# Attention scores as products of short operands, and a triangular inverse from blocks of 4, in a three-block network

## The reference

```python
def compress(kv, pe, w1, w2):
    blocks = (kv[:, blk] + pe).reshape(B, nc, CMP_LEN * NSA_KV_DIM)
    return jax.nn.silu(blocks @ w1) @ w2
...
s_w = (jnp.einsum('bnqhd,bnkd->bnhqk', q.reshape(B, n_qb, Q_BLOCK, H, dh), kw).astype(f32) * scale
       - slopes[None, None, :, None, None] * dist[None, :, None].astype(f32))
p_w = masked_softmax(s_w, mask[None, :, None])
...
s = jnp.einsum('bqhid,bkhid->bhiqk', qb, k).astype(f32) * scale
```

```python
r_t, w_t, k_t, v_t, a_t, b_t = inp
sa = jnp.einsum('bhvk,bhk->bhv', S, a_t)
S = S * w_t[:, :, None, :] + sa[..., :, None] * b_t[:, :, None, :] + v_t[..., :, None] * k_t[:, :, None, :]
y = jnp.einsum('bhvk,bhk->bhv', S, r_t)
```

## Time and profile before

| | |
|---|---|
| median of three runs | 4650.26 us (4645.92 to 4656.61) |
| profiled execution | 4649.78 us, span 4648.0 us |
| mean granted clock of PE | 0.957 |
| PE busy | 4284.1 us, 92% of the span |
| DVE, ACT, POOL busy | 41%, 29%, 25% |
| compress stage | 441.4 to 470.1 us |
| NSA attention | 470.1 to 682 us |
| diff attention | 682 to 868 us |
| recurrence, first to last right side | 1507.7 to 1904.0 us |

### The profile page before, as it was taken

One profiled execution on the slowest core, in us unless ns is written; L12 is line 12 of the kernel. 1 busy time (PEld: TensorE's weight loads), 2 busy tenths in 40 slices (PEclk: granted clock), 3 DMA queues, 4 the chain that ended last, 5 costly groups with the idle time before them and its releaser, 6 DMA issues. The chain is left out here.

```text
span 4648.0 us, 53906 instructions
## 1 busy us (share of the span) xinstructions
PE 4284.1 (92%) x21558; PEld 3501.7 (75%) x21558; DVE 1886.4 (41%) x3289; ACT 1343.2 (29%) x2357; POOL 1154.4 (25%) x575
## 2 busy tenths in 40 slices
PE   8999999879995888699999999999999999967897
PEld 6888777656775887468888877888788888856776
DVE  3022666652595665435424424000133333346433
ACT  3121333432313443421001012112244444343112
POOL 2220100331152666222222212212111111122313
PEclk9999999879997999899999999999999999978899
DMA  3243111331523110311111112333333333266422
GB/s 123 102 157 102 34 27 26 118 97 50 208 87 99 42 31 17 110 46 46 55 46 46 55 37 89 113 138 104 90 84 104 104 107 95 67 218 191 154 82 91
DMA packets 276997, 417.23 MB, mean 90 GB/s; under 512 B 50439, under 2 KB 184120, under 8 KB 270862
## 3 DMA queue, kind: packets, MB, share of 16 engines
q1 hardware_dynamic: 221022, 313.20, 21.8%
q10 hardware_dynamic: 53104, 94.92, 5.5%
q0 software_dynamic: 2624, 5.68, 0.5%
HBM read 290.31 MB, written 123.40 MB: 89 GB/s over the span
## 5 line engine op out<-in xcount | busy, mean ns | idle before, releaser
L163 POOL TENSOR_TENSOR weights_wlow<-weights_raw,weights_whigh 128x1024 fp32r<-128x1024 f32 (+1 forms) x236 | 695.6, 2969 | 2450.3 <-ACT weights_whigh L154 2450.3
L154 ACT ACTIVATE weights_whigh<-weights_raw 128x1024 fp32r<-128x1024 f32 (+1 forms) x236 | 266.6, 1164 | 1170.8 <-PE acc L313 787.8
L313 PE MATMUL acc<-h_high_half,weights_whigh 128*128 128x512 f32 x1408 | 556.8, 395 | 20.9 <-POOL weights_wlow L163 17.1
L313 PE MATMUL acc<-h_low_half,weights_whigh 128*128 128x512 f32 x1408 | 553.7, 393 | 0.0
L313 PE MATMUL acc<-h_high_half,weights_wlow 128*128 128x512 f32 x1408 | 553.5, 393 | 0.0
L313 PEld LDWEIGHTS acc<-h_high_half,weights_whigh 128*128 128x128 f32 x1408 | 266.0, 189 | 89.2 <-POOL weights_wlow L163 18.4
L3575 PE MATMUL acc<-h_high_half,weights_whigh 128*128 128x512 f32 x768 | 331.3, 431 | 0.0
L313 PEld LDWEIGHTS acc<-h_high_half,weights_wlow 128*128 128x128 f32 x1408 | 265.9, 189 | 59.3 <-issue 1.0
L313 PEld LDWEIGHTS acc<-h_low_half,weights_whigh 128*128 128x128 f32 x1408 | 265.6, 189 | 59.3
L3575 PE MATMUL acc<-h_low_half,weights_whigh 128*128 128x512 f32 x768 | 302.2, 393 | 0.0
L3575 PE MATMUL acc<-h_high_half,weights_wlow 128*128 128x512 f32 x768 | 300.8, 392 | 0.0
(11 more groups left out here) (555 smaller groups left out, 8238.9 us busy)
## 6 DMA issues: line engine op xcount, KB each, us to landing
weights_raw<-w_cols SPq DMA_DIRECT2D x94, 512.0 KB, 4.8
weights_raw<-w_ff SPq DMA_DIRECT2D x64, 512.0 KB, 3.7
weights_raw<-w_rows SPq DMA_DIRECT2D x30, 1024.0 KB, 7.2
att<-gated_result_sb SPq DMA_DIRECT2D x96, 130.0 KB, 2.2
merge_o_sb<-att SPq DMA_DIRECT2D x24, 520.0 KB, 6.6
rows<-norm_square ACTq DMA_DIRECT2D x48, 256.0 KB, 2.1
weights_raw<-w_out SPq DMA_DIRECT2D x24, 512.0 KB, 3.8
cols<-first_out ACTq DMA_DIRECT2D x40, 256.0 KB, 2.0
```

Source lines behind the costliest of these rows:

```text
L154: self.core.nc.scalar.activation(high[p][:, half * (KC // 2):(half + 1) * (KC // 2), :], raw[half], ACT.Copy).then_inc(self.core.sem("roun ...
L163: self.core.nc.gpsimd.tensor_tensor(low[p][:, hs, :], raw[half], high[p][:, hs, :].bitcast(F32), ALU.subtract).then_inc(self.core.sem("wei ...
L313: mm = nc.tensor.matmul(core.acc[b][:, :], wt[p][:, k, c * P:(c + 1) * P], h[:, k, half * HALF:(half + 1) * HALF], start=first, stop=final)
```

## The change

**Scores.** Queries and keys of both attentions are rounded to fp32r ("short"), and what the rounding drops (the "low") is kept as a second short operand. q k is then q_high k_high + q_high k_low + q_low k_high, and the three terms lie below each other on the rows of the operands. In NSA (head size 64) a chunk takes two products: [q_high; q_high] with [k_high; k_low] on 128 rows, and [q_low; slope, slope] with [k_high; two parts of the position] on 66. In diff (head size 32) a chunk takes one, of 3 x 32 + 6 = 102 rows. The masks and the identity in front of them are short too. Turn, mix and softmax stay as they are.

The rows are made by loading the same columns two or three times. In `compress` the clearing of the loaded tiles is gone; ACT rounds keys and masks (`round`) when all loads are there, between its Silus of i = 0 and i = 1, and the compressed keys at the end; DVE makes the keys' lows; POOL splits the queries of heads 0 and 1, and later each loaded head (`split`), for which PE waits at a head's first step. In the diff attention ACT and DVE make the first score set of head 0 ahead of all else, POOL the rest.

**Recurrence.** D now holds 4x4 blocks, so one power is enough: `SOLVE` is P2t, X and then four levels to 64; 19 steps stand for 22. The last doubling, 64 to 128, is not made: `unknowns` solves the first 64 positions, `second_half` multiplies them by the square that joins the halves (`across`, copied by DVE behind step 0), DVE adds (`raise_second`), and `unknowns` solves the second 64.

```diff
@@ attention
-                if j:
-                    pe.wait_ge(sem[f"att_loaded_{p}"], at[f"att_loaded_{p}"] + 16 * nl * j)
...
+                    begun.wait_scores(pe, it, k)
...
+            begun.scalar_first(a)
...
+            begun.vector_first(v)
...
+                pool.wait_ge(sem[f"att_loaded_{p}"], at[f"att_loaded_{p}"] + 16 * len(loads(it, p)) * j)
+                begun.split(pool, it)
...
             if constants:
+                for it in range(2):
+                    begun.split(pool, it)
                 constants.load(pool)
@@ class SparseTiles
+    def round(self, a):
+
+        act, last = self.core.nc.scalar.activation, slice(HD, HD + 2)
+        self.loaded(a)
+        for b in ("slc", "win"):
+            act(self.both[b][:, :], self.raw[b], ACT.Copy)
+            act(self.place[b][0:HD, :], self.raw[b][0:HD, :], ACT.Copy)
+            act(self.place[b][last, :], self.raw_place[last, :], ACT.Copy)
+        act(self.place["cmp"][last, :], self.raw_centre[last, :], ACT.Copy)
+        act(self.diff.ident[:, :], self.core.ident[:, :], ACT.Copy)
+        act(self.diff.late[:, :], self.raw_late[:, :], ACT.Copy)
+        act(self.early[:, :], self.raw_early[:, :], ACT.Copy)
+        act(self.unseen[:, :, :], self.raw_unseen[:, :, :], ACT.Copy).then_inc(self.core.sem("cmp_rounded"), 1)
...
+    def split(self, pool, it):
+
+        nc, p, done = self.core.nc, it % 2, self.core.sem("head_steps")
+        nc.gpsimd.tensor_copy(self.q[p][:, :], self.raw_q[p][:, :]).then_inc(done, 1)
...
+        nc.gpsimd.memset(self.low[p][HD:HD + 2, :].bitcast(F32), float(SLOPES[2 * it]) * HD ** 0.5).then_inc(done, 1)
...
+        nc.gpsimd.tensor_tensor(self.low[p][0:HD, :], self.raw_q[p][0:HD, :], self.q[p][0:HD, :].bitcast(F32),
+                                ALU.subtract).then_inc(done, 1)
...
+    def keys(self, p, t, b, c0, c1):
+
+        q = slice(t * P, (t + 1) * P)
+        return [(self.q[p][:, q], self.both[b][:, c0:c1]), (self.low[p][0:HD + 2, q], self.place[b][0:HD + 2, c0:c1])]
@@ compress
                     nc.scalar.activation(hid[i][:, m, :], core.acc[2 * i + m][:, 0:NCMP], ACT.Silu).then_inc(active, 1)
+                if i == 0:
+                    nsa.round(a)
+            nsa.round_compressed(a)
@@ class DiffTiles
+    ROWS = 3 * (HD // 2) + 6
...
+            for raw, at, constant in ((self.raw_q, DQ, d["diff_slope_parts"][it]), (self.raw_k, DK, d["position_thrice"][:, :])):
+                of = cols[ds(it * HD + (at + part * i), part), :]
+                out += [(raw[p][i][part * c:part * (c + 1), :], of) for c in range(3)]
+                out.append((raw[p][i][3 * part:self.ROWS, :], constant))
...
+    def wait_scores(self, pe, it, k):
+
+        if it == 0 and k == 0:
+            pe.wait_ge(self.core.sem("first_low"), 2)
+        if (it, k) == (0, NT) or it and k == 0:
+            pe.wait_ge(self.core.sem("head_steps"), 3 * HEADS + 8 * it + 4)
@@ Recurrence
-STEPS = 22
+STEPS = 19
...
+SOLVE = [("P2t", "D", "Dt"), ("X", "P2t", "X")] + [
+    step for i in range(4) for step in (("Xt", None, "X"), ("Y", f"M{i}", "X"), ("X", "Xt", "Y"))]
...
+        for c in range(4):
+            for b in range(2):
+                e = slice(c * P + b * HD, c * P + (b + 1) * HD)
+                at = 4 * b + c
+                mm = nc.tensor.matmul(core.acc[4][:, e], across[:, at * HD:(at + 2) * HD], self.u[0:HD, e],
+                                      start=True, stop=True)
...
+                if j == 0:
+                    ins.then_inc(self.sig(f"by_vector{b}"), 1)
+                    ins = nc.vector.tensor_copy(self.across[t % 2][:, 1 + 4 * b:5 + 4 * b, :], self.four(acc)[0:HD, :, HD:])
...
                         if j == 1 and t:
-                            w.unknowns(pe, t - 1)
+                            w.unknowns(pe, t - 1, 0)
...
                         if j == 3 and t:
-                            w.outputs(pe, t - 1)
+                            w.second_half(pe, t - 1)
...
+                            w.unknowns(pe, t - 1, 1)
+                        if j == 9 and t:
+                            w.outputs(pe, t - 1)
+                        if j == 12 and t:
                             w.means(pe, t - 1)
-                        if j == 8 and t:
+                        if j == 15 and t:
                             w.variances(pe, t - 1)
```

More of the change, by code:

```diff
@@ L1133 @@
 HALF_BLK = 16
+SLOPES = np.array([2.0 ** (-8.0 * (n + 1) / 8) for n in range(8)], np.float32)
+DIFF_SLOPES = SLOPES[1::2]
 class WindowTiles:
@@ L1208, in load, with loaded @@
+        out += [(val[b][:, :, :], rows[:, v:v + HD].rearrange("(t p) e -> p t e", p=P)) for b, v in (("slc", VSLC), ("win", VWIN))]
+        return out + [(self.valid[:, :], d["has_compressed"][:, :]), *self.head(1, 1)]
     def load(self, sp):
-        sp.wait_ge(self.core.sem("cmp_cleared"), len(self.padded))
         for to, of in self.pairs():
             sp.dma_start(to, of).then_inc(self.core.sem("fetched"), 16)
+    def loaded(self, eng):
+        eng.wait_ge(self.core.sem("fetched"), 16 * len(self.pairs()))
@@ L1283, in nsa_attention @@
         att = d["att1"]
-        q, kT, val, late, early, unseen, valid = nsa.q, nsa.kT, nsa.val, nsa.late, nsa.early, nsa.unseen, nsa.valid
+        val, late, early, unseen, valid, ident = nsa.val, diff.late, nsa.early, nsa.unseen, nsa.valid, diff.ident
         def steps(p):
@@ new lines, in loaded, with lows, split @@
+    def loaded(self, eng):
+        eng.wait_ge(self.core.sem("diff_loaded"), 16 * 2 * len(self.head(0, 0)))
+    def lows(self, p, i):
+        part = HD // 2
+        for tile, raw, c in ((self.q[p][i], self.raw_q[p][i], 1), (self.k[p][i], self.raw_k[p][i], 2)):
+            low = tile[part * c:part * (c + 1), :]
+            yield low, raw[part * c:part * (c + 1), :], low.bitcast(F32)
+    def split(self, pool, it):
+        nc, p, part = self.core.nc, it % 2, HD // 2
+        if it == 0:
+            self.loaded(pool)
+        done = self.core.sem("head_steps")
+        for i in range(2) if it else (1,):
+            at, rows = 3 * HEADS + 8 * it + 4 * i - 4, slice(0, self.ROWS)
+            q_low, k_low = (slice(part * c, part * (c + 1)) for c in (1, 2))
+            q, k, raw_q, raw_k = self.q[p][i], self.k[p][i], self.raw_q[p][i], self.raw_k[p][i]
+            nc.gpsimd.tensor_copy(q[rows, :], raw_q[rows, :]).then_inc(done, 1)
+            pool.wait_ge(done, at + 1)
+            nc.gpsimd.tensor_copy(k[rows, :], raw_k[rows, :]).then_inc(done, 1)
+            pool.wait_ge(done, at + 2)
+            nc.gpsimd.tensor_tensor(q[q_low, :], raw_q[q_low, :], q[q_low, :].bitcast(F32), ALU.subtract).then_inc(done, 1)
+            pool.wait_ge(done, at + 3)
+            nc.gpsimd.tensor_tensor(k[k_low, :], raw_k[k_low, :], k[k_low, :].bitcast(F32), ALU.subtract).then_inc(done, 1)
+            pool.wait_ge(done, at + 4)
@@ L1375, in shape_constants @@
     i = np.arange(P)
-    slopes = np.array([2.0 ** (-8.0 * (n + 1) / 8) for n in range(8)], f)
     c = {}
@@ L2350, in __init__ @@
         tile = lambda n: [sb(f"{n}{b}", [P, RW]) for b in range(2)]
-        self.m = {n: tile(n) for n in ("D", "Dt", "Nt", "P2", "P2t", "Nk", "M0", "M1", "M2")}
-        self.m |= {"P4": self.m["D"], "P4t": self.m["Dt"], "P8t": self.m["P2t"], "Xt": self.m["Nt"], "Y": self.m["P2"]}
+        self.m = {n: tile(n) for n in ("D", "Dt", "Nt", "P2t", "Nk", "M0", "M1", "M2")}
+        self.m |= {"Xt": self.m["Dt"], "Y": self.m["D"], "M3": self.m["P2t"]}
+        self.across = [sb(f"across{p}", [HD, 9, HD]) for p in range(2)]
         self.late = {n: [tile(f"{n}{p}_") for p in range(2)] for n in ("Rb", "Rk", "X")}
@@ L2461, in right_side, with unknowns @@
         mm.then_inc(self.sig("rhs_sum"), 1)
-    def unknowns(self, pe, t):
+    def unknowns(self, pe, t, i):
         nc, core = self.core.nc, self.core
-        pe.wait_ge(self.sig("rhs"), t + 1)
-        for b in range(2):
-            self.after_vector(pe, t, b, 21)
+        if i:
+            pe.wait_ge(self.sig("second"), t + 1)
+        else:
+            pe.wait_ge(self.sig("rhs"), t + 1)
+            for b in range(2):
+                self.after_vector(pe, t, b, 18)
         for c in range(4):
@@ L3050, in _ @@
                 nc.vector.memset(w.eps[:, :], 64e-5)
+                for p in range(2):
+                    nc.vector.memset(w.across[p][:, 0, :], 0.0)
                 nc.vector.memset(w.S[:, :, :], 0.0).then_inc(sig("state"), 1)
```

353 lines of the change are left out of this document (205 added, 148 removed), and 5 rows, old and new, of the table SOLVE.

## The result

The changed kernel takes 4599.12 us (median of four, 4592.76 to 4605.41) against 4649.16 for the kernel before in the same session: the ratio is 0.9891, with a 95% interval of 0.9879 to 0.9903. So it is 50 us faster, where 50 us slower had been forecast. It is near the number of rival B (4590 to 4609), but the clock did not stay at full speed as B has it.

The account below looks back on a forecast made before the run. PE, busy 92% of the span, was taken as the bound. From 4649.8 us, NSA -8, diff +61, compress +7.6, diff's start +3.6 and recurrence -14 gave 4700 us; range 4655 to 4790.

Parts of the forecast that it names:

- rival B: Both attentions: PE at full clock throughout, total 4609 or 4590 us; chance 0.19.
- The clock: Both attentions: thinner PE work starts at half clock; NSA returns to full clock, diff stays at 0.50.
- the +61: Diff attention: four heads at half clock, 61.5 us each instead of 45.4, less 3 for the start: 61 us slower.
- I take the pair: Both attentions: a short product of 128 columns costs 0.23 us, like the pair of fp32 passes before.
- the cheap reading: Both attentions: a short product of 128 columns costs one short pass, 0.116 us, saving 9.3 us per NSA head.
- NSA's -8: NSA attention: cheaper heads give -13 us, a longer half-clock start in the first head +5, together 8 us faster.
- Compress +7.6: Compress stage: ACT's rounding waits for all loads and delays the second Silus, 7.6 us slower.
- Diff's start +3.6: Start of diff attention: two roundings and one subtraction ahead of PE's first score, 3.6 us slower.
- Recurrence -14: Whole recurrence: shorter tiles and a longer tail sum to 14 us faster, bounds -35 to +10.
- The head of a tile: Recurrence, start of a tile: 14.4 us, on DVE before and after, so removing PE's outputs only leaves PE idle.
- the outputs behind step 9: Recurrence tile: outputs moved behind the turn of step 9 fill waits and push the rest by 4.7 us.
- the tail: End of the recurrence: a chain of second half, add and unknowns makes it 5 us longer.

Follow-up runs that it names:

- e2: The kernel before with the change to the recurrence alone, attention scores as before: 4624.54 us, 0.9942 of the kernel before.
- e1: The kernel before with the change to the attention scores alone, recurrence as before: 4628.26 us, 0.9954 of the kernel before.
- e3: The changed kernel with POOL's two output operations moved behind the four levels' masks of a tile: 4625.76 us, 0.9951 of the kernel before.
- e8: The kernel before with POOL's masks waiting until DVE has evacuated the fifth score product: 4640.56 us, 0.9977 of the kernel before.

## Why the prediction was wrong, point by point

**The clock, the step that decided the sign.** "diff, where one product stands for four passes, I expect to stay at 0.50 throughout" failed: it is at 0.87, and NSA at 0.88, not the 1.00 in heads 1 to 3 that was expected there. Nor is it B, "full clock in both". The argument took the start of a stage as the only place where the clock can fall and what follows as one mean load. A head is not one load: the clock comes up in its heavy steps and falls in its light ones. From first to last exp diff took 153 us, where the 176 before and the +61 make 237. The Trainium skill's rule (TensorE: Matmul & The Clock Gate, section "What's actually happening"), with PE's busy time as the activity, does no better: in 530 to 540 PE is busy 10.00 of 10 at a clock of 0.50.

**The price of short products.** "I take the pair", 0.23, failed; it is 0.11, the lower bound. At that price PE's work in a head falls by the 9.3 and 13 us of the cheap reading. The sum's own heads do not quite follow from its savings: 52.3 less 9.3 or 2.5 is 43.0 or 49.8, not 44.8 or 49.0. The cheap heads at full clock, 44.8 and 38, would have saved some 60 us in both attentions; the line above puts it at 72.

**NSA's -8** was -16 (190.0 against 205.6 from first to last exp), and that it came out on the right side is partly luck: two errors met, cheaper products and a clock that fell in each head.

**Compress +7.6** was right in size and mechanism: +8.7 to the first exp, loads at 466.2, Silus at 474.2. **Diff's start +3.6** was +6.2: from NSA's last exp to diff's first 12.7 us against 6.5. DVE's two subtractions took 2.05 and 3.25 us beside POOL's first split, and only one of 1.2 had been counted; the clock was at 0.50. POOL's cast is 1.04 us, and its splits held nobody up in later heads, as forecast.

**Recurrence -14.** The stage, between the large products on either side, takes 515.4 us instead of 547.8 in the profile, -32; the medians give -26 (e2) and -29 (the changed kernel against e1). Inside a tile one term was wrong: "The head of a tile, now 14.4 us to 1578.93, is on DVE in both". It was forecast at 15 us and is 10.0. The others hold: P2t and X 6.6 (6.9), levels 6.63 each, the outputs behind step 9 push by 5.3 (4.7). The head needed two things, and e3 and e8 show both: the outputs gone from PE, and POOL's masks not beside DVE's shifts. The second comes from POOL's output operations, which now run at the start of a tile; the forecast did not look at them and read the shifts' 1.49 us as their cost. Around the tiles the errors went both ways: tile 0 gained 4.3 and not 6, tile 1 lost 1.9 (58.8 us), tiles 2 to 5 gained 6.8 or more each and not 0.8, tiles 6 and 7 came down to 49.2 and not 51.1, and the tail cost 12.4 and not 5: PE worked through most of it at half clock, a second place where the forecast did not look for the clock.

**The sum.** By the profiles it is -32 for the attentions with diff's start, +9 for compress, -32 for the recurrence, -1 elsewhere in the first block, and +4 in the third block, together -53. No instruction has changed in the third block: it takes 2694.1 us in the profile before, the shortest of the seventeen kernels here, and 2695.7 to 2700.7 in the others, so the 4 us are scatter.

## What to carry to other kernels

When the work of an engine under a clock gate gets thinner, look at it step by step: the clock can fall over a run of light steps or behind one wait, and the steps behind pay 0.4 us for each us at half clock, here by estimate 40 us of a gain of 72. A filler that keeps the clock up costs its own passes, here as much as it gave. A duration in the trace is a cost plus the waits inside it: before a chain is summed, look at what the engine that shares its ports does at that moment, and try moving that first. A reordering is not free either: with light steps between heavy ones this one-step-ahead pipeline ran emptier.

## What the runs showed of the hardware

A product of 128 columns of short operands takes 0.11 us at full clock, on 66 or 128 rows. A DVE operation with two SBUF operands and a POOL operation that reads SBUF exclude each other. When POOL came first, DVE's 0.47 us became 1.49 and 1.22 became 3.36, and a DVE cast of 64x1024 took 2.83; when DVE came first, POOL's 2.51 for two became 4.74. And two kernels with the same instructions in a stage, but for one split moved, took 351 and 383 us for it, at mean clocks of 0.88 and 0.79.
